# Experts under four first keys: taken out of the per-token gathers and computed for all tokens on TensorE

## The reference, cut to what matters

```python
def chunk(c):                                    # 128 tokens at a time
    q = (xc @ wq).reshape(B, C, PEER_HEADS, PEER_DQ)            # 8 heads
    s1 = einsum('bchd,nd->bchn', q[..., :half], keys1)          # 128 first keys
    s2 = einsum('bchd,nd->bchn', q[..., half:], keys2)          # 128 second keys
    v1, i1 = top_k(s1, 16); v2, i2 = top_k(s2, 16)
    cand = (v1[..., :, None] + v2[..., None, :]).reshape(B, C, PEER_HEADS, 256)
    sc, ci = top_k(cand, 16)
    e = i1[ci // 16] * 128 + i2[ci % 16]         # 16 experts of 16384
    g = softmax(sc, axis=-1)
    a = gelu(einsum('bchkd,bcd->bchk', U[e], xc))
    return einsum('bchk,bchkd->bcd', g * a, V[e])
```

## Time and profile before

| | us |
|---|---|
| median of 3 runs | 2159.53 (2157.35 to 2160.74) |
| the profiled execution | 2158.93 |
| its span, first to last instruction | 2157.2 |

### The profile page before, as it was taken

The page is one execution under the profiler, slowest core; times in us unless marked ns, Lnnn a source line. Parts: engine busy times, 40 slices in busy tenths (PEclk is TensorE's granted clock), DMA queues, the critical chain, the costliest instruction groups (busy, mean ns, idle before and its releaser), DMA issues.

```text
span 2157.2 us, 22090 instructions
## 1 busy us (share of the span) xinstructions
PE 1864.7 (86%) x6535; PEld 1096.5 (51%) x6535; DVE 1286.2 (60%) x2142; ACT 588.8 (27%) x1064; POOL 728.2 (34%) x636
## 2 busy tenths in 40 slices
PE   9999999999999999999977777777777777777777
PEld 7888887777788786544423222222222222222222
DVE  5544556787866556776356556556556556546444
ACT  5544445555544443111111111111111111111101
POOL 2000011110000002755455445445455545545542
PEclk9999999999999999999999999999999999999999
DMA  7556743434456578999999999999999999999997
GB/s 266 190 186 198 225 150 108 146 108 136 139 180 236 188 237 309 398 412 403 421 422 420 422 421 422 422 422 422 422 422 422 422 422 422 422 422 421 422 422 329
DMA packets 164609, 699.82 MB, mean 324 GB/s; under 512 B 15633, under 2 KB 25905, under 8 KB 98257
## 3 DMA queue, kind: packets, MB, share of 16 engines
q0 software_dynamic: 74176, 537.35, 60.1%
q1 hardware_dynamic: 90384, 161.89, 23.4%
q10 hardware_dynamic: 2, 0.01, 0.0%
HBM read 697.10 MB, written 2.10 MB: 324 GB/s over the span
## 4 chain that ended last, share of the span: by engine, by line
PE 50%; DMA 38%; issue 5%; DVE 5%; POOL 1%; ACT 0%; DVEq 0%; POOLq 0%; ACTq 0%
DMA v_ring<-in_peer_v_dram,idx_v 31%; PE banks L1253 10%; PE banks L788 9%; PE banks L790 9%; PE banks L789 9%; DMA big<-in_peer_u_dram,idx_u 7%; PE banks L1222 4%; PE banks L764 1%; PE banks L1143 1%; DVE big L2358 1%; POOL v_ring L643 1%; DVE mx L1990 1%; DVE ws L1832 1%; DVE att L1987 1%; PE banks L1190 1%
## 5 line engine op out<-in xcount | busy, mean ns | idle before, releaser
L1253 PE MATMUL banks<-v_ring,kxT 128*128 128x512 f32 x1920 | 885.4, 605 | 266.7 <-DMA v_ring<-in_peer_v_dram,idx_v 265.7
L2358 DVE SCALAR_TENSOR_TENSOR big<-big,xn 128x2048 f32<-128x2048 f32 x256 | 586.9, 2293 | 417.4 <-DMA big<-in_peer_u_dram,idx_u 409.0
L1253 PEld LDWEIGHTS banks<-v_ring,kxT 128*128 128x128 f32 x1920 | 348.3, 190 | 801.3 <-ACT kxT L1736 390.2
L634 POOL DMA_INDIRECT big<-in_peer_u_dram,idx_u x256 | 369.9, 1445 | 203.8 <-DVE big L2358 109.2
L1832 DVE TENSOR_TENSOR ws<-wraw,ws 128x1024 fp32r<-128x1024 f32 (+1 forms) x248 | 294.6, 1194 | 210.2 <-ACT ws L1373 208.2
L643 POOL DMA_INDIRECT v_ring<-in_peer_v_dram,idx_v x240 | 283.0, 1179 | 404.5 <-PE banks L1253 360.4
L1736 ACT ACTIVATE kxT<-ident,ga 128x128 f32<-128x128 f32 x240 | 95.3, 401 | 954.6 <-PE banks L1253 951.8
L1373 ACT ACTIVATE ws<-wraw 128x1024 fp32r<-128x1024 f32 (+1 forms) x248 | 254.6, 1033 | 220.2 <-PE banks L790 202.8
L788 PE MATMUL banks<-ws,xr 128*128 128x512 f32 x736 | 294.5, 400 | 3.1 <-DVE ws L1832 2.2
L790 PE MATMUL banks<-ws,xr 128*128 128x512 f32 x736 | 287.3, 390 | 0.0
L789 PE MATMUL banks<-ws,xr 128*128 128x512 f32 x736 | 287.2, 390 | 0.0
(11 more groups left out here) (325 smaller groups left out, 1485.3 us busy)
## 6 DMA issues: line engine op xcount, KB each, us to landing
wraw<-in_w_in_dram SPq DMA_DIRECT2D x152, 512.0 KB, 3.5
wraw<-in_w_out_dram SPq DMA_DIRECT2D x32, 512.0 KB, 4.0
wraw<-in_w_xkv_dram SPq DMA_DIRECT2D x16, 512.0 KB, 6.8
wraw<-in_w_branch_da_dram SPq DMA_DIRECT2D x16, 512.0 KB, 3.9
wraw<-in_w_branch_nsa_dram SPq DMA_DIRECT2D x16, 512.0 KB, 4.1
wq<-in_peer_wq_dram SPq DMA_DIRECT2D x10, 512.0 KB, 14.5
wraw<-in_w_xq_dram SPq DMA_DIRECT2D x8, 512.0 KB, 3.6
wb<-in_peer_wq_dram SPq DMA_DIRECT2D x8, 512.0 KB, 6.9
```

Source lines behind the costliest of these rows:

```text
L634: nc.gpsimd.indirect_dma_start(u_ring[:, r, :], None, peer_u[0], bass.IndirectOffsetOnAxis(ap=idx_u[par][:, j:j + 1], axis=0)).then_inc(u_ ...
L1253: last = nc.tensor.matmul(V_BANKS[c][n], diag[:, r, :], v_ring[:, r, n * NW:(n + 1) * NW], start=(first and j == 0), stop=(final and j == ...
L2358: V.scalar_tensor_tensor(out=u_ring[:, r, :], in0=u_ring[:, r, :], scalar=1.0, in1=xn3[:, par, :], op0=ALU.mult, op1=ALU.mult, accum_out=d ...
```

## The change

Experts 0 to 511 are those of the first keys 0 to 3 (`RES = 4` times 128 second keys). Their rows are 4 MB of U and 4 MB of V.

1. Gathers. From unit 1 on, a pick with a first key under 4, unless it is the 16th of its token and head, gets 16384 added to its index. All gathers carry a bounds check at 16383 that is not an error, so that row is not to be moved. Its weight in `ga` is set to zero, and `dot` writes its product to another tile (`grow`) instead of over the U row. Unit 0 stays as it was.
2. Dots for all tokens. SP loads the 512 rows of U into `res`. While PE does the V slots of unit 2, it also transposes them (four 128x128 a step, 16 steps), ACT copies each step out of PSUM (`chunk_copy`), and PE multiplies with the normed input (`d_products`, two products of 128x128 by 128x512 a step). ACT then takes the gelu of both chunks (`d_res`).
3. Gates for all tokens. For units 1 to 15 DVE marks which of the 512 sums of key scores lie above the 16th candidate (`gate_mask`), ACT takes the exponentials (`gate_exps`), DVE weighs and sums them over heads (`gate_add`). For units 1 to 3 this is done in DVE's U unit 3 from kept scores (`held_route`).
4. Values for all tokens. SP loads the 512 rows of V over those of U. Beside V slots of units 13 and 14 PE transposes the weights and adds 16 products to each chunk's banks. For that, DVE empties bank 0 of a chunk into `h` first (`w_of`, which also multiplies gates and `d_res`), and all four banks of chunk 1 after its unit 1. In `v_step_beside` the four transposes follow slot 3, two products follow each of slots 5 to 9 and one each of slots 10 to 15.

In the diff below, the parts are ordered by engine; the other two fetches and `decode` for unit 0 change as or stay as said above. In ACT's steps of V unit 2, `gate_exps(3)` and `gate_exps(4)` stand at j = 8 and 12.

```diff
+RES = 4
+ONCE = 16
 # SP
             sp.wait_ge(wq_used, RAWS)
+            for e in range(RES):
+                if e == RES - 1:
+                    for hh in range(2):
+                        sp.wait_ge(tp_free[hh], (GQ + 14) // 2 + 2)
+                sp.dma_start(res[e], peer_u[0][e * NKEYS:(e + 1) * NKEYS, :]).then_inc(res_landed, 16)
             sp.dma_start(gfin[:, :], norm_final_g.partition_broadcast(P)).then_inc(gfin_landed, 16)
+            sp.wait_ge(uT_ready, ONCE + KT)
+            for e in range(RES):
+                sp.dma_start(res[e], peer_v[0][e * NKEYS:(e + 1) * NKEYS, :]).then_inc(res_landed, 16)
 # POOL
                 nc.gpsimd.indirect_dma_start(u_ring[:, r, :], None, peer_u[0],
-                                             bass.IndirectOffsetOnAxis(ap=idx_u[par][:, j:j + 1], axis=0)).then_inc(u_landed[r], 16)
+                                             bass.IndirectOffsetOnAxis(ap=idx_u[par][:, j:j + 1], axis=0),
+                                             bounds_check=EXPERTS - 1, oob_is_err=False).then_inc(u_landed[r], 16)
 # PE
-            v_step(1, 1, first=True)
-            with pe.Fori(1, PH - 1) as i:
+            v_step(1, 1, first=True, ends=4)
+            def u_transposes(t):
+                if t == 0:
+                    pe.wait_ge(res_landed, ONCE + 16 * RES)
+                    pe.wait_ge(bank_free, ONCE + 1)
+                else:
+                    pe.wait_ge(chunk_ready, ONCE + t - 1)
+                for e in range(RES):
+                    last = nc.tensor.transpose(B[2 + t % 2][:, e * P:(e + 1) * P], res[e][:, t * P:(t + 1) * P], ident[:, :])
+                last.then_inc(uT_ready, 1)
+            def d_products(t):
+                pe.wait_ge(chunk_ready, ONCE + t + 1)
+                for c in range(C):
+                    last = nc.tensor.matmul(B[c], xf[:, t, c * P:(c + 1) * P], chunk[:, t % 2, :], start=(t == 0), stop=(t == KT - 1))
+                last.then_inc(d_used, 1)
...
+            for j in range(PK):
+                v_slot(2, 0, j)
+                if j >= 1:
+                    u_transposes(j - 1)
+                if j >= 2:
+                    d_products(j - 2)
+            u_transposes(KT - 1)
+            for t in range(KT - 2, KT):
+                d_products(t)
+            pe.wait_ge(d_ready, ONCE + C)
+            v_step(3, 1, first=True)
+            with pe.Fori(2, PH - 2) as i:
                 v_step(i * 2, 0)
                 v_step(i * 2 + 1, 1)
-            v_step(UNITS - 2, 0, final=True)
+            v_step(UNITS - 4, 0, ends=1)
+            v_step_beside(UNITS - 3, 1, 0, 1)
+            v_step_beside(UNITS - 2, 0, 1, 4)
 # ACT
+            def chunk_copy(t):
+                act.wait_ge(uT_ready, ONCE + t + 1)
+                if t >= 2:
+                    act.wait_ge(d_used, ONCE + t - 1)
+                A(chunk[:, t % 2, :], B[2 + t % 2], ACT.Copy).then_inc(chunk_ready, 1)
...
+            act.wait_ge(ga_ready, 3)
+            gate_exps(1)
+            for j in range(PK):
+                diagonals(0, 2, range(j, j + 1))
+                if j >= 2:
+                    chunk_copy(j - 2)
+                if j == 3:
+                    gate_exps(2)
+                if j == 4:
+                    route_softmax(4)
...
+            for t in range(KT - 2, KT):
+                chunk_copy(t)
+            act.wait_ge(d_used, ONCE + KT)
+            for c in range(C):
+                A(d_res[:, c, :], B[c], ACT.Gelu, scale=rstd[:, 6 + c:7 + c]).then_inc(d_ready, 1)
+            gelu(1, 3)
+            beside(1, 3)
+            with act.Fori(2, PH - 2) as i:
 # DVE, decode
+                    V.scalar_tensor_tensor(out=keep[:, :], in0=e12[:, 0, :], scalar=float(RES), in1=keep[:, :], op0=ALU.is_lt, op1=ALU.mult)
+                    link(V.scalar_tensor_tensor(out=abf[:, 0, :], in0=e12[:, 0, :], scalar=float(NKEYS), in1=e12[:, 1, :],
+                                                op0=ALU.mult, op1=ALU.add))
+                    V.scalar_tensor_tensor(out=idx_u[par][:, :], in0=keep[:, :], scalar=float(EXPERTS), in1=abf[:, 0, :],
+                                           op0=ALU.mult, op1=ALU.add).then_inc(ready, 1)
+                    link(V.tensor_scalar(keep[:, :], keep[:, :], -1.0, 1.0, ALU.mult, ALU.add))
 # DVE, gates
+            def gate_mask(first4, second, thr, neg_max):
+                V.tensor_scalar(bias4[:, :], first4, neg_max, None, ALU.add).then_inc(bias_ready, 1)
+                for e in range(RES):
+                    V.tensor_scalar(g_over[:, e * P:(e + 1) * P], second, first4[:, e:e + 1], thr, ALU.add, ALU.is_gt)
+            def gate_add(u, c, over_sum, first=False):
+                dve.wait_ge(dense_exp, ONCE + u)
+                link(V.scalar_tensor_tensor(out=g_all[:, c, :] if first else g_one, in0=g_one, scalar=over_sum, in1=g_over, op0=ALU.mult, op1=ALU.mult))
...
+                    link(V.tensor_tensor(g_all[:, c, :], g_all[:, c, :], g_one, ALU.add))
 # DVE, step
+                    if isinstance(u, int) and u == 3:
...
+                        if j == 4:
+                            dve.wait_ge(v_used, 2 * 16 + RING)
+                            V.tensor_tensor(h[:, 1, :], psum[:, 0:4 * NW], h[:, 1, :], ALU.add).then_inc(bank_free, 1)
...
+                    if weigh_last and j == 11:
+                        gate_mask(wk[:, 0, 0:RES], wk[:, 1, :], sc16[:, PK - 1:PK], nsc[:, :])
+                    if isinstance(u, int) and u == UNITS - 2 and j == 4:
+                        w_of(0, UNITS - 3)
                 if weigh_last:
+                    gate_add(u + 1, 1 - par, exs[:, 1:2])
                     weigh(u, par)
```

More of the change, by code:

```diff
@@ L266, in block_program @@
         half_mix = big[:, 2048:2560]
+        res = [res_t[:, e, :] for e in range(RES - 1)] + [later[:, 4096:6144]]
+        chunk = product_t[:, 0:2 * NW].rearrange("p (b n) -> p b n", b=2)
+        g_all = product_t[:, 2 * NW:4 * NW].rearrange("p (c n) -> p c n", c=C)
+        g_one, g_over = big[:, 9 * D:9 * D + NW], big[:, 9 * D + NW:9 * D + 2 * NW]
+        d_res = big[:, 7 * D:7 * D + 2 * NW].rearrange("p (c n) -> p c n", c=C)
+        wT = big[:, 7 * D + 2 * NW:7 * D + 4 * NW].rearrange("p (c e n) -> p c e n", c=C, e=RES)
         vc_now = arena[0:2 * CMP_ROWS, 6016:6144]
@@ new lines, in res_products, with v_step_beside @@
+            def res_products(c, ms):
+                if ms[0] == 0:
+                    pe.wait_ge(wT_copied, ONCE + c + 1)
+                    pe.wait_ge(res_landed, ONCE + 32 * RES)
+                for m in ms:
+                    e, n = m // 4, m % 4
+                    nc.tensor.matmul(V_BANKS[c][n], wT[:, c, e, :], res[e][:, n * NW:(n + 1) * NW], start=(m == 0), stop=False)
+            def v_step_beside(u, c, dense, ends):
+                m = 0
+                for j in range(PK):
+                    v_slot(u, c, j, False, ends)
+                    if j == 3:
+                        w_transposes(dense)
+                    if j >= 5:
+                        count = 2 if j < 10 else 1
+                        res_products(dense, range(m, m + count))
+                        m += count
@@ L1751, in _, with gate_exps @@
             diagonals(1, 1, range(12, PK))
-            with act.Fori(1, PH - 1) as i:
-                for par, u in ((0, i * 2), (1, i * 2 + 1)):
[L1755 to L1759, removed]
+            def gate_exps(u):
+                act.wait_ge(bias_ready, ONCE + u)
+                act.wait_ge(dense_done, ONCE + u - 1)
+                second = scores[:, u * 256 + P:u * 256 + 2 * P] if isinstance(u, int) and u < 4 else wk[:, 1, :]
+                for e in range(RES):
+                    last = A(g_one[:, e * P:(e + 1) * P], second, ACT.Exp, bias=bias4[:, e:e + 1])
+                last.then_inc(dense_exp, 1)
@@ new lines, in chunk_copy, with wT_copy, beside @@
+            def chunk_copy(t):
[3 more added lines that the diff above has]
+                A(chunk[:, t % 2, :], B[2 + t % 2], ACT.Copy).then_inc(chunk_ready, 1)
+            def wT_copy(c):
+                act.wait_ge(wT_ready, ONCE + c + 1)
+                A(wT[:, c, :, :], V_BANKS[c][0].rearrange("p (e n) -> p e n", e=RES), ACT.Copy).then_inc(wT_copied, 1)
+            def beside(par, u, dense=None):
+                act.wait_ge(ga_ready, u + 1)
+                diagonals(par, u, range(0, 5))
+                route_softmax(u + 2)
+                diagonals(par, u, range(5, 7))
+                if dense is not None:
+                    wT_copy(dense)
+                diagonals(par, u, range(7, 12))
+                gate_exps(u + 2)
+                diagonals(par, u, range(12, PK))
+                gelu(1 - par, u + 1)
@@ L1762, in _ @@
+            wT_copy(1)
+            diagonals(0, UNITS - 2, range(7, PK))
             gelu(1, UNITS - 1)
```

88 lines of the change are left out of this document (75 added, 13 removed).

## The result

The changed kernel takes 2199.5 us at the median (2197.3 to 2201.3), the kernel before, run beside it, 2158.4: a ratio of 1.0189, interval [1.0171, 1.0207]. So it is slower, as forecast, by 41 us where 24 were worked out; the time lies inside the range of 2160 to 2204, 16 us above the value of 2183.5.

The account below looks back on a forecast made before the run. The expert layer was taken to last as long as its DMA work, plus time with the queue dry. 10.0 + 27.4 - 13.4 = +24.0 us gave 2183.5 us against the median, range 2160 to 2204.

Parts of the forecast that it names:

- rivals A to D: A rows pool, 2164.8 (0.16); B only bytes count, 2146.2 (0.09); C dropped rows cost, 2196.9 (0.08); D POOL bounds, 2298 (0.07).
- the forecast case: The prediction's main case for the whole kernel: 2183.5 us, own range 2175 to 2193, chance 0.52.
- C: Gathers: rows out of bounds still cost a row's time, +37.4 us, 2196.9 us; chance 0.08.
- E: V unit 2: PE's steps or the restart of gathers take longer than composed, 2190 to 2205 us; chance 0.08.
- The stall: End of V unit 2: DVE and POOL wait for the late gelu, +27.4 us, 10.0 V rows and 17.4 idle queue.
- The one long wait of 35 to 45 us: Sign in the profile: one DVE wait for ACT's `act_u` near the end of V unit 2.
- the gates are long done: V unit 2: while DVE waits at `weigh(3)`, `held_add` and the gates were taken as already finished.
- Rows read once: Plain loads of U and V rows, 32 rows an engine each: +10.0 us for U, 10.0 for V within the stall.
- Rows spared: Gathers of units 1 to 15: the least relieved engine is spared 43 rows at 0.311 us, -13.4 us.
- rival A: Gathers: saved rows pool over all engines, -32.1 instead of -13.4 us, 2164.8 us; chance 0.16.
- more than 1% apart from 4.97: Sign against the prediction: V slots outside the stall differing by over 1% from a 4.97 us distance.
- Steady units: Units outside the stall: DVE's, ACT's and PE's added work is covered by idle time and queue, cost 0, up to 3.

Follow-up runs that it names:

- the first repair: The changed kernel with ACT's gelu of U unit 3 moved right after the 16th diagonal of V unit 2: 2197.8 us, ratio 1.0179 to the kernel before.
- loads_only: The kernel before plus the change's plain loads of 4 MB of U and 4 MB of V, used by nothing, no row spared: 2177.2 us, ratio 1.0087.
- drop_only: The kernel before with the same rows not gathered as in the changed one and nothing put in their place: 2140.7 us, ratio 0.9919.
- all_fixed: The changed kernel with ACT's steps in V unit 2 reordered and DVE's loop written out: 2166.5 us, ratio 1.0049 to the kernel before.
- gates_early: The changed kernel with exponentials of units 3 and 4 after V unit 2's slots 5 and 8, gelu after slot 11: 2182.6 us, ratio 1.0116 to before.
- pad18_ahead56: The kernel before with 18 unused copies per unit in DVE's loop and 56 more once ahead of it: 2178.7 us, ratio 1.0099.
- pad18: The kernel before with 18 unused copies per unit in DVE's loop, none ahead of it: 2160.7 us, ratio 1.0011.
- each_engine: The kernel before with indices of 16 partitions (0, 4, .. 28 and 64, 68, .. 92) out of bounds in units 1 to 15: 2026.8 us, ratio 0.9392.

## Why the prediction was right or wrong

- Direction and range were right, and the frame was: with a queue that never rests, time is DMA work plus the time in which the queue is dry. None of the rivals A to D came true. But the time is also outside the forecast case's own 2175 to 2193. It lies in the range only because that was drawn up to 2204 for C and E, so it was held by a margin meant for other causes; that part is luck.
- The stall: 27.4 us forecast for V unit 2, 26.6 measured; 17.4 of idle queue, 18.6 measured. PE's step 5.67, 5.59 measured. Undoing the waits gave back 16.9 us. The one long wait of 35 to 45 us that was to be seen came as two, 14.9 and 26.2 us. One sentence of this step was wrong: "the gates are long done". `held_add(3)` waited 14.9 us, since ACT is in step with PE there. It cost nothing on top: both waits eat into the same 30 gathers, and what the first held back was still to be moved later. The end of the dry time was set by the last transposes and SP's loads behind them, which is why the first repair failed.
- Rows read once: +20.0 forecast, +18 by themselves (`loads_only`).
- Rows spared: -13.4 forecast for before and after the stall together; for the whole run -16 expected and -17 measured by `drop_only`. In the changed kernel with DVE unrolled, the part after the stall took 982.7 us instead of 994.1, -11.4, where 13.1 were taken and 12.1 follow from the map in fours. The reasoning against rival A was right: engines don't share, or by 1% only. Of the two readings that were to tell it, one was wrong: the DMA share stayed at 1.01 in `drop_only` and fell only where an engine had nothing at all. The slots told it instead. Between 1215 and 2060 us, 128 of the 171 distances between V slots in `drop_only` are 4.92 to 5.02 us, as before, and 34 are 4.60 to 4.75. A slot stands for a gather of U and one of V, so 16 rows an engine, and 15/16 of 4.97 is 4.66: most slots keep their length, and some lose just one row. That is the pattern of a slowest engine that is only now and then spared, where a shared saving would shorten every slot a little. The sign "more than 1% apart from 4.97" was therefore drawn too narrow. PE in order of time in `drop_only`, at three slots as before and then at three of which the last two are close:

```profile
1175.08 3.70 PE L1256 MATMUL banks<-v_ring,kxT 128*128 128x512 f32 x8 [1.28 <-DMA v_ring<-in_peer_v_dram,idx_v]
1180.03 3.70 PE L1256 MATMUL banks<-v_ring,kxT 128*128 128x512 f32 x8 [1.25 <-DMA v_ring<-in_peer_v_dram,idx_v]
1185.01 3.69 PE L1256 MATMUL banks<-v_ring,kxT 128*128 128x512 f32 x8 [1.28 <-DMA v_ring<-in_peer_v_dram,idx_v]
...
1309.01 3.69 PE L1256 MATMUL banks<-v_ring,kxT 128*128 128x512 f32 x8 [1.26 <-DMA v_ring<-in_peer_v_dram,idx_v]
1313.65 3.70 PE L1256 MATMUL banks<-v_ring,kxT 128*128 128x512 f32 x8 [0.95 <-DMA v_ring<-in_peer_v_dram,idx_v]
1318.31 3.69 PE L1256 MATMUL banks<-v_ring,kxT 128*128 128x512 f32 x8 [0.96 <-DMA v_ring<-in_peer_v_dram,idx_v]
```

- The step that failed is "Steady units", priced at "0, up to 3". It counted the busy time of DVE's added operations, which is indeed covered, and not that they put more code into the loop and ahead of it. Four waits of 5.8 us came of it, at the one place in each trip where DVE has waited for ACT already (4.7 us) and POOL is waiting for DVE; together they outlast the queue. That is 15 us by the unrolled run, nearly all of the 17 us between the forecast 24 and the measured 41. Rival E had the price, 2190 to 2205, but not the mechanism: PE's step and the restart were not longer than composed.
- A bound of the sum is off: by the prediction's own terms the lower bound's transposes end at 9.9 + 14 x 4.97 + 0.52 = 80.0, not 80.8. The range doesn't rest on it.
- Left open: `all_fixed` is 7 us above before, where `loads_only` and `drop_only` sum to +1. About 2 us are idle queue in V unit 2 (a share of 0.91 from 1140 to 1160 us, as in `gates_early`). For the rest, no run tells it apart.

## What to carry to other kernels

Where gathers fill the DMA engines, count rows per engine, and take the engine that is spared least: here the poorest of 16 engines was spared about half the mean, 52 rows against 107, and 64 were paid for, so the idea loses even with both losses mended. An instruction moved behind a lockstep of two other engines takes their pace; place it by when its inputs are ready and by who stands behind its reader. And when a loop's body or the code ahead of it grows, look at the first instruction after its jump back: idle time that the profile puts down to issue was code being fetched here, and it cost 15 to 18 of its 23 us because another engine was waiting for that instruction.

## What the runs showed of the hardware that was not expected

- A loop's jump back cost DVE 5.8 us under full DMA load (`pad18_ahead56`), and nothing with the same loop starting 56 operations earlier (`pad18`).
- Leaving one engine of 16 without gather work shortened the run by 0.4%, while the rate fell from 422 to 399 GB/s: the others went 1% faster at the most.
- A row out of bounds costs its engine next to nothing: with 1/8 of the rows left out on each engine, slots came every 4.37 instead of 4.97 us, 12.1% less where 12.5% would be a free row (`each_engine`).
- Rows left out unevenly shorten single slots by a whole row, from 4.97 to 4.66 us, and leave the others as they were (`drop_only`).
